# Index columns in two half-contraction units, bias tables moved to the first feed-forward stage, rotary angles in PSUM

## The reference

```python
proj = h @ w_in[l]                       # 1024 x 10052
aq, ak, av, iq, ik, iw, glu_in, cc_in, sb_in, gate_in = split(proj)
# iq: 4 heads x 64, ik: 64, iw: 4  -> the 324 "index" columns
qa = partial_rope(rms_norm(aq), positions)   # angles = position * frequency
qi = partial_rope(iq, positions)
u  = causal_dwconv(glu_a * sigmoid(glu_b), cb_conv_w[l])   # 31 taps
```

## Time and profile before

| | |
|---|---|
| median of 3 runs | 1786.15 us (1782.39 to 1786.66) |
| profiled execution, its span | 1784.4 us |
| PE busy, share | 1726.8 us, 97% |
| DVE busy, share | 1227.4 us, 69% |
| ACT busy, share | 931.5 us, 52% |
| POOL busy, share | 124.5 us, 7% |
| mean granted TensorE clock | 0.983 |
| DMA mean | 171 GB/s, 305.75 MB |

### The profile page before, as it was taken

How to read it: one execution, slowest core, us unless ns; L and a number is a source line. 1 busy time by engine, 2 the same in 40 slices (tenths; PEclk the granted TensorE clock), 3 DMA queues, 4 the chain that set the end, 5 groups by cost and what they waited for, 6 DMA issues and landing times.

```text
span 1784.4 us, 31735 instructions
## 1 busy us (share of the span) xinstructions
PE 1726.8 (97%) x13416; PEld 1631.4 (91%) x13416; DVE 1227.4 (69%) x1927; ACT 931.5 (52%) x1291; POOL 124.5 (7%) x35
## 2 busy tenths in 40 slices
PE   7999999999999999999999998889999999999998
PEld 6998999899989999999999898769998899889986
DVE  6994946798649877567887466877554655666553
ACT  5446655554445545664554355756443665655442
POOL 2620300000004603000000000000000000000000
PEclk9899999999999999999999989999999999999999
DMA  8684546556564654646465555324655476436552
GB/s 231 184 202 131 185 129 218 176 166 204 200 199 138 187 166 142 190 142 212 153 202 191 191 157 154 119 72 148 206 190 197 165 214 169 131 118 204 197 203 71
DMA packets 248636, 305.75 MB, mean 171 GB/s; under 512 B 9266, under 2 KB 223630, under 8 KB 248495
## 3 DMA queue, kind: packets, MB, share of 16 engines
q1 hardware_dynamic: 235959, 289.66, 50.6%
q10 hardware_dynamic: 12536, 14.06, 4.1%
HBM read 299.51 MB, written 4.19 MB: 170 GB/s over the span
## 4 chain that ended last, share of the span: by engine, by line
PE 77%; DVE 14%; DMA 3%; ACT 3%; issue 2%; ACTq 0%; DVEq 0%; SPq 0%
PE psum L477 23%; PE psum L478 23%; PE psum L479 23%; DVE wlo L453 3%; DVE psum L1488 3%; DMA raw<-in_w_in 1%; DVE work L1620 1%; PE psum L2489 1%; DMA work<-in_a_w_v 1%; PE psum L2515 1%; PE psum L2501 1%; DMA raw<-in_b_w_q 1%; DVE work L2288 1%; DVE work L2304 1%; DVE work L1634 1%
## 5 line engine op out<-in xcount | busy, mean ns | idle before, releaser
L445 ACT ACTIVATE whi<-raw 128x2048 fp32r<-128x2048 f32 (+2 forms) x277 | 524.1, 1901 | 366.2 <-PE psum L479 258.5
L453 DVE TENSOR_TENSOR wlo<-raw,whi 128x2048 fp32r<-128x2048 f32 x249 | 567.0, 2282 | 197.0 <-PE psum L479 161.9
L477 PE MATMUL psum<-hT,whi 128*128 128x256 f32 x1890 | 525.3, 278 | 0.0
L478 PE MATMUL psum<-hT,whi 128*128 128x256 f32 x1890 | 524.2, 277 | 0.0
L479 PE MATMUL psum<-hT,wlo 128*128 128x256 f32 x1890 | 523.7, 277 | 0.0
L477 PEld LDWEIGHTS psum<-hT,whi 128*128 128x128 f32 x1890 | 356.3, 189 | 0.0
L479 PEld LDWEIGHTS psum<-hT,wlo 128*128 128x128 f32 x1890 | 356.2, 188 | 0.0
L478 PEld LDWEIGHTS psum<-hT,whi 128*128 128x128 f32 x1890 | 356.1, 188 | 0.0
L453 POOL TENSOR_TENSOR wlo<-raw,whi 128x2048 fp32r<-128x2048 f32 (+1 forms) x28 | 123.3, 4405 | 573.9 <-ACT whi L445 394.9
L477 PE MATMUL psum<-whi,hidden 128*128 128x512 f32 x352 | 137.3, 390 | 1.0 <-issue 1.0
L479 PE MATMUL psum<-whi,hidden 128*128 128x512 f32 x352 | 137.0, 389 | 0.0
(11 more groups left out here) (383 smaller groups left out, 3371.7 us busy)
## 6 DMA issues: line engine op xcount, KB each, us to landing
raw<-in_w_in SPq DMA_DIRECT2D x78, 1024.0 KB, 5.7
raw<-in_ffn_w_up SPq DMA_DIRECT2D x44, 1024.0 KB, 5.1
raw<-in_w_ffn_gate SPq DMA_DIRECT2D x22, 1024.0 KB, 5.3
raw<-in_w_ffn_up SPq DMA_DIRECT2D x22, 1024.0 KB, 5.4
raw<-in_w_ffn_down SPq DMA_DIRECT2D x22, 1024.0 KB, 5.0
raw<-in_ffn_w_down SPq DMA_DIRECT2D x22, 1024.0 KB, 4.9
raw<-in_b_w_q SPq DMA_DIRECT2D x12, 1024.0 KB, 6.3
raw<-in_a_w_in SPq DMA_DIRECT2D x10, 1024.0 KB, 5.4
```

The costliest lines, as they stand in the source:

```text
L445: act.activation(part(whi, n, HIGH_SLOTS), part(raw, n, RAW_SLOTS), ACT.Copy).then_inc(high_made, 1)
L453: eng.tensor_tensor(part(wlo, n, LOW_SLOTS), part(raw, n, RAW_SLOTS), part(whi, n, HIGH_SLOTS).bitcast(F32), ALU.subtract).then_inc(stream ...
L477: nc.tensor.matmul(dst, left[0], right[0], start=first, stop=False)
L478: nc.tensor.matmul(dst, left[0], right[1], start=False, stop=False)
```

## The change

1. The index columns become two units of 324 columns by half the contraction (512 rows) each. PE takes both banks before the first, adds four contraction tiles from each unit, and releases the first by `unit_used`. ACT evicts each bank by one activation of 324 columns.
2. The bias tables leave the setup and the mixer. In the first feed-forward up stage ACT issues their two loads at the start (after a DVE fill of the table), PE makes one table after each of units 6, 8, 10 and 12, DVE copies one at the end of pairs 4 to 7, ACT stores one after the high part of pairs 5 to 8, and waits for the stores at the stage's end.
3. The rotary angles lie in PSUM bank 7. Their order on DVE stays.

```diff
-        u += column_units(w, W_IDX, W_GLU, "P")
+        u += [(w[i * 512:(i + 1) * 512, W_IDX:W_GLU], "P") for i in range(2)]
...
+            lifted = bank(7)[:, 2 * TT * 24:3 * TT * 24].rearrange("p (t f) -> p t f", f=24)
...
-            v_link(dve.tensor_scalar(turns, s_, 1.0 / (2 * math.pi), magic, ALU.mult, ALU.add))
-            v_link(dve.tensor_scalar(turns, turns, -magic, None, ALU.add))
+            v_link(dve.tensor_scalar(lifted, s_, 1.0 / (2 * math.pi), magic, ALU.mult, ALU.add))
+            v_link(dve.tensor_scalar(turns, lifted, -magic, None, ALU.add))
...
-        tab = region(8192, 4, SPAN)
-        ang = region(10000, 2 * TT, 24)
+        tab = region(24832, 4, SPAN)
+        ang = bank(7)[:, 0:2 * TT * 24].rearrange("p (t f) -> p t f", f=24)
...
-            soon = [(cst[:, 2 * P:], consts[:, 2 * P:]), (onehot[0:BUCKETS + 1, :], onehots),
-                    (work[0:BUCKETS, 24800:24800 + QH], a["rel_bias_2"]),
+            soon = [(cst[:, 2 * P:], consts[:, 2 * P:]),
...
+        def load_distances(act):
+
+            act.dma_start(onehot[0:BUCKETS + 1, :], onehots).then_inc(distance_load.sem, 16)
+            act.wait_ge(bias_cleared.sem, bias_cleared.at(1))
+            act.dma_start(work[0:BUCKETS, 24800:24800 + QH], a["rel_bias_2"]).then_inc(distance_load.sem, 16)
+
+        def distance_row(pe, base, n):
+
+            if n == 0:
+                pe.wait_ge(distance_load.sem, distance_load.at(32))
+            nc.tensor.matmul(bank(base + n)[0:QH, 0:SPAN], work[0:BUCKETS + 1, 24800:24800 + QH],
+                             onehot[0:BUCKETS + 1, n * SPAN:(n + 1) * SPAN], start=True, stop=True) \
+              .then_inc(distance_full.sem, 1)
...
+        def store_distance(act, n):
+
+            act.wait_ge(distance_copied.sem, distance_copied.at(n + 1))
+            home = band_dram[:, n - 1] if n else table_dram
+            act.dma_start(home[:, :, 0:SPAN], spread(tab[0:QH, n, :], 1, ROWS)).then_inc(side_store.sem, 16)
...
+                    if tables and n in (6, 8, 10, 12):
+                        distance_row(pe, turned, n // 2 - 3)
+                if tables:
+                    pe.wait_ge(distance_copied.sem, distance_copied.at(4))
                 end(pe)
...
                 begin(act)
+                if tables:
+                    load_distances(act)
...
                     high(c)
+                    if tables and 5 <= c < 9:
+                        store_distance(act, c - 5)
+                if tables:
+                    act.wait_ge(side_store.sem, side_store.at(64))
                 end(act)
...
+                if tables:
+                    dve.memset(work[0:BUCKETS + 1, 24800:24800 + QH], NEG).then_inc(bias_cleared.sem, 1)
...
                     make_lows(dve, n0 + 2 * c + 5)
+                    if tables and 4 <= c < 8:
+                        copy_distance(dve, turned, c - 4)
...
+                    if n in INDEX:
+                        half = n - INDEX[0]
+                        if half == 0:
+                            whole_turned(pe)
+                            own_bank(p)
+                            own_bank(p + 1)
+                        for j in range(TT):
+                            for k in range(4):
+                                mm = three_passes(bank(j)[:, 0:IDX_COLS],
+                                                  [row_tile(v, 4 * half + k)[:, j * P:(j + 1) * P] for v in hT],
+                                                  [v[:, k, :] for v in w], half == k == 0, half == 1 and k == 3)
+                            if half:
+                                mm.then_inc(bank_full.sem, 1)
+                        if half == 0:
+                            mm.then_inc(unit_used.sem, 1)
+                            release_unit(unit_used, 1)
+                        else:
+                            release_unit(bank_full, p + 1)
+                        return
...
-                    if l == 0 and n == RAW:
-                        distance_rows(pe)
...
+                    elif n in INDEX:
+                        t = n - INDEX[0]
+                        if t == 0:
+                            make_high(act, n0 + n + HIGH_SLOTS + 1)
+                        act.wait_ge(bank_full.sem, bank_full.at(product_of[n] + 1))
+                        act.activation(idx[:, t, :], bank(t)[:, 0:IDX_COLS], ACT.Copy).then_inc(dense_free[t].sem, 1)
+                        if t:
+                            make_high(act, n0 + n + HIGH_SLOTS + 1)
...
-                    if l == 0 and n in (6, 9, 12, 15):
-                        i = n // 3 - 2
-                        act.wait_ge(side_free.sem, side_free.at(i + 1))
-                        home = band_dram[:, i - 1] if i else table_dram
-                        act.dma_start(home[:, :, 0:SPAN], spread(tab[0:QH, i, :], 1, ROWS)) \
-                           .then_inc(side_store.sem, 16)
...
                 long_conv(0, 10, 18)
-                if l == 0:
-                    copy_distances(dve)
                 long_conv(0, 18, LONG)
```

More of the change, by code:

```diff
@@ L336, in two_part_transformer @@
         side_store = signal("side_store")
+        bias_cleared = signal("bias_cleared")
+        distance_load = signal("distance_load")
+        distance_full = signal("distance_full")
+        distance_copied = signal("distance_copied")
         keys_copied = signal("keys_copied")
@@ L726, in _ @@
                 pool.memset(praw, 0.0).then_inc(operand_ready.sem, 1)
-                pool.memset(work[0:BUCKETS + 1, 24800:24800 + QH], NEG).then_inc(operand_ready.sem, 1)
             @block.scalar
@@ L733, in _ @@
                 act.dma_start(early[0:KT, :], a["g_mix"][0].rearrange("(t p) -> t p", p=P)).then_inc(gain_load.sem, 16)
-                act.wait_ge(operand_ready.sem, operand_ready.at(3))
+                act.wait_ge(operand_ready.sem, operand_ready.at(2))
                 for dst, src in soon:
@@ L762, in _ @@
                 end(dve)
-            operand_ready.close(3)
+            operand_ready.close(2)
             gains_turned.close(1)
@@ L790, in copy_parameters, with copy_distance @@
             v_link(dve.tensor_copy(par[:, 4 * P:PARAM_TILES * P], bank(3)[:, 0:(PARAM_TILES - 4) * P]))
[L792 to L797, removed]
+        def copy_distance(dve, base, n):
+            dve.wait_ge(distance_full.sem, distance_full.at(n + 1))
+            dve.tensor_copy(tab[0:QH, n, :], bank(base + n)[0:QH, 0:SPAN]).then_inc(distance_copied.sem, 1)
+        def store_distance(act, n):
+            act.wait_ge(distance_copied.sem, distance_copied.at(n + 1))
+            home = band_dram[:, n - 1] if n else table_dram
+            act.dma_start(home[:, :, 0:SPAN], spread(tab[0:QH, n, :], 1, ROWS)).then_inc(side_store.sem, 16)
         def add_rows_product(lhsT, nk, base, kind, gain):
@@ L863, in add_rows_product, with ffn_up_stage @@
             return base ^ 4
-        def ffn_up_stage(conv, turned, gain):
+        def ffn_up_stage(conv, turned, gain, tables=False):
             pairs = FT // 2
@@ L1012, in ffn_up_stage @@
             hand_over(pairs)
+            if tables:
+                bias_cleared.close(1)
+                distance_load.close(32)
+                distance_full.close(4)
+                distance_copied.close(4)
+                side_store.close(64)
             if conv is not None:
@@ L1066, in mixer_stage @@
             n0, count, rows, RAW = len(stream.freed), 48, raw_T["mixer"], 4
+            INDEX = (RAW, RAW + 1)
             OUTS = (32, 33, 38, 39, 44, 45, 46, 47)
@@ L1740, in mixer_stage @@
             gate_scaled.close(2)
+            unit_used.close(1)
             if l == 0:
@@ L1745, in mixer_stage @@
                 rows_scaled.close(1)
-                side_store.close(64)
                 side_load.close(side_loads[0])
-                side_full.close(5)
-                side_free.close(4)
+                side_full.close(1)
             hand_over(4)
@@ L2756, in _ @@
                               .then_inc(x_load[h].sem, 16)
-                        sp.wait_ge(operand_ready.sem, 3)
+                        sp.wait_ge(operand_ready.sem, 2)
                     if n == 2:
```

7 lines of the change are left out of this document (1 added, 6 removed).

## The result

The changed kernel takes 1772.6 us (median; 1769.77 to 1773.61), the kernel before 1784.9 beside it: ratio 0.9939, 95% interval 0.9924 to 0.9955. That is 12.3 us less by the medians; 11.1 were forecast. The profiled execution has a span of 1771.8 us, 12.6 less than before.

The account below looks back on a forecast made before the run. PE, busy for 97% of the span, bounds the kernel. Terms of -5.1 - 1.1 - 6.9 - 2.7 - 0.4 + 2.7 + 0.4 + 2.0 = -11.1 us give span 1773.3, median 1775.0 us; range 1768.5 to 1785.

Parts of the forecast that it names:

- The second means: Layer 0's second channel means: without the fourth store, unit 20's load lands early and PE's wait goes, -6.9 us.
- the half clock behind it: Layer 0, from the second means on: the low clock after the wait goes too, -2.7 us.
- VectorE's lead: Layer 0's second convolution: DVE ends it 10.1 us sooner through faster angles and fewer copies, 7.6 left after POOL.
- Layer 0, index: Layer 0's index units: idle of 6.6 us, halves 6.9, low clock costing 1.7; net -5.1 us.
- the table passes until 49.81, and the 48 of 68 columns until 59.63: Layer 0 before: tables, then 68-column matmuls mostly at half clock; new pair 6.9 us in place of 5.5 + 9.8.
- Layer 1: Layer 1's index units: idle of 4.95 us, gain 2.5 less 1.4 for the clock, -1.1 us.
- The start: Start of the kernel: 198 KB of one-hot rows no longer travel ahead of x, -0.4 us.
- The feed-forward stage: Layer 0's feed-forward: table passes +2.7, DVE's late start +0.4, stores delaying weight loads +2.0 us.
- the late start: Layer 0's feed-forward: ACT's two DMA issues make DVE start 1.05 us late, 0.65 of it covered, +0.4 us.
- A: Layer 0's feed-forward: stores starve weights, 8.4 us and up to 2.5 for the clock, 1783 us; chance 0.18.
- B: Layer 0's feed-forward: store rounds take 16.7 us against PE's 11.7, losing 19 to 21, 1792 us; chance 0.06.
- rival C: Layer 0's mixer: angles don't speed up and DVE's chain stays late, +2.8 us, 1778 us; chance 0.08.

Follow-up runs that it names:

- part 2 alone: Kernel before with only the bias tables moved to the first feed-forward stage, index units and angles as before: ratio 0.9968, 1776.7 us.
- part 3 alone: Kernel before with only the rotary angles moved to PSUM: ratio 0.9987, 1781.6 us.
- the fastest kernel: Changed kernel with the index products in banks 4 and 5 and the four bias-table products in a row after unit 6: 1758.04 us.
- the kernel with other banks: Changed kernel with the two index products in banks 4 and 5, which are free by then: 1762.05 us.
- parts 2 and 3: Changed kernel with its index columns in units of 256 and 68 columns as before: ratio 0.9957, 1776.1 us.

## Why the prediction was right

Point by point, by its own steps:

- **The second means.** -6.9 forecast, -7.0 measured, and the half clock behind it -2.2 against -2.7. The mechanism holds: part 2 alone takes the wait to 1.3, part 3 alone leaves 6.2. ScalarE's squares ended at 120.70, 1.9 us before TensorE began the means at 122.63; "two us before PE asks" was the forecast.
- **VectorE's lead was right by luck.** The step gave 10.1 us at the second convolution's end, from 8.7 for the angles and 1.9 for the copies, less 0.5. Measured are 9.9 (102.84 to 92.96). But the angles gave back 6.3 only, since the conversion ahead of them grew from 0.17 to 2.65, and the earlier start gave 1.8, which the step had left out.
- **Layer 0, index.** -5.1 forecast, -5.8 measured up to the first means. The idle was 6.73 (6.6). The two halves took 8.66, of which 7.14 is the full-clock price (6.9) and 1.5 the low clock (1.7). Units 6 to 14 took 49.33 in place of 52.63: 2.2 of it is the clock, and 1.1 a closer pitch (0.1142 in place of 0.1183) that no step foresaw. The number was right; that it belonged to the index units was not shown by it: they give it only where the tables are gone and the angles early. On top of part 2 alone they cost 0.2%, alone too. The step "the table passes until 49.81, and the 48 of 68 columns until 59.63" is one term of two parts that need each other. The Trainium skill, *TensorE: Matmul & The Clock Gate*, "HAM oscillation — how this bites in real kernels", says that waits between bursts of matmuls put the engine back to the low clock. The trace agrees for the two long idles (6.73 and 4.94 us): the clock was low behind each. Behind the two of 1.61 us it was not, but it was behind one of 2.16 us in the fastest kernel, and in five of the fourteen profiles behind the 1.9 us that TensorE waits for its first weights, each time with a wait of 0.4 to 0.5 us shortly ahead of it. So no length of an idle at which the clock stays up is shown. The prediction also read the wait of the kernel before a little long: the clock fell 5.1 us into it (130.6 to 135.7), not 5.4.
- **Layer 1.** -1.1 forecast, -1.1 to the first means, by luck. Two errors cancel: the halves took 9.28 us, where 6.9 and 1.4 for the clock were forecast (full clock is 7.14, so the low clock cost 2.1), and the close pitch behind them gave 1.2 back.
- **The start** was mis-sized: -0.4 for the bytes at 310 GB/s, -1.8 measured, of which the load alone makes 1.57. From 5 to 9 us the queues move 372 GB/s in the changed kernel, 325 with the load put back and 316 in the kernel before. So it costs the others more than its own bytes.
- **The feed-forward stage**, +5.1 forecast, +5.3 measured, by other terms. The stores cost TensorE nothing (2.0 forecast): its only wait for weights in the up stage is 0.23 us, at 364.98. With the slower pitch of the unit behind it (0.118 in place of 0.114) this makes 0.7, the most that the late start (0.4) can have cost. The tables cost 4.5, not 2.7: the distance of a pair of units is 12.09 with a table and 10.96 without, 1.13 each. In the earlier trace rows the same pass pairs took 0.69 in a row. The prediction priced a single from a row; a single has 0.75 from its start to the next matmul, and the unit behind it runs at 0.118 a matmul in place of 0.114, which adds 0.2; 0.2 is left. The two terms, 4.5 and 0.7, make up the stage's difference.
- **Starved weights (rivals A and B).** The mechanism is real, but single stores leave it hidden. After each store the next high part waited 3.4 to 4.9 us for its load, and the lead of the parts covered it. With twice the store bytes the stage was 20.3 us longer than the changed kernel's. That is the size given to B (19 to 21), but not its shape: B had four stalls behind single stores, and here one of 12.6 us at unit 20 and one of 3.2 make most of it. (By B's own terms, 20 less 7 and up to 8 more, it was 13 to 21.) This run bears out that the lead kept A away, as the prediction said against it; the share of ScalarE's order is argued only. The Trainium skill, *DMA: Bandwidth & Descriptors*, "Issuing engines are not separate DMA queues", has the queues interleave. The measurement decides here: the windows of 100 and 99 GB/s, which is about the rate of the store alone (768 KB in 8 us), and ScalarE's wait of 11.2 us for weights behind two stores against 3.45 behind one, show that a load behind such a store gets nearly nothing until it ends.
- **Angles (rival C).** They did speed up, to 0.21 and 0.22. Had they not, the price would have been some 6.5 to 8.5 and not 2.8: the step asked only when unit 20's load goes out, and overlooked that ScalarE evicts VectorE's second convolution before the bank of unit 14. The gate that VectorE's end hits first stood some 24 us earlier (unit 14 began at 98.98, the means at 122.63).

The forecast thus holds in total, and for the means by its reason. The start missed by -1.4 us, the tables by +1.8, the stores by -2.0 and layer 0's index stretch by -0.7. With the small ones the sum is 1.5 off the profiles' difference and 1.2 off the medians', so the closeness of the total is in part luck. One reading was incomplete: besides the 6.9 us TensorE has two more waits before 460 us, 5.9 for a parameter load and 4.8 for x, both at the start, and of these only the second had a term.

## What to carry to other kernels

Two edits that touch the same stretch are to be priced together and apart: here the new units alone made it 0.2% slower and, on top of the two others, about 0.2% faster (0.9957 to 0.9939, with intervals that overlap). A wait that an edit makes unavoidable should be looked at for what the engine could write to instead; putting two products in free banks was worth nearly as much as the whole change. When a late engine is followed to its consumers, list every wait on it in the order of time, and not only the one that shows now.

## What was not expected of the hardware

- Matmuls of one shape (128 x 256, same operands) run at one of two pitches at full clock, 0.1177 to 0.1185 or 0.1132 to 0.1145 us, and keep it for a unit or several: 3.5%. In layer 1, units 6 to 14 took 49.3 us behind 324-column units in every kernel that had them and 52.0 or 53.3 behind 68-column ones, of which 1.4 to 2.9 is low clock. In the feed-forward stage the slow pitch stands in the unit behind each singled table and ends with that unit; with the tables in a row it stands once. It also stood behind short waits (0.23 us in the feed-forward stage, 0.47 in the kernel with other banks) but not behind those of 1.61. What sets it was not found.
- The clock stays low for different times in the same code: the 68-column matmuls of layer 0 took 6.54, 7.21, 8.66 and 9.82 us in four profiles (part 2, part 3, parts 2 and 3, before; in two of them the table passes stood just ahead).
- A matmul of 324 columns has a pitch of 0.149 us, against 0.114 to 0.118 for 256.
- In layer 0's 6.7 us idle the clock fell 3.1 us into the idle, in the wait of the kernel before 5.1 us into it.
- Angles in PSUM take VectorE's small operations out of GpSimd's way (4.6 to 0.2 us); an integer conversion of 128 x 2 elements that stayed in SBUF took 0.17 in two of the fourteen profiles and 0.49 to 4.27 in the others, 2.65 in the changed kernel.
